# Four attentions in one kernel: another form of nsa's compression, some high halves on ScalarE, and moved steps in swa, diff and fox

## The reference

```
def compress(t, pe, w1, w2):                       # nsa, for keys and for values
    blk = (t[:, :, cidx] + pe).reshape(b, g, n_cmp, CMP_LEN * hd)   # 31 blocks of 32 tokens, step 16
    return jax.nn.gelu(blk @ w1) @ w2              # 2048 -> 256 -> 64
q, k, v, f_logit = jnp.split(x @ w_in, ...)        # fox; log_sigmoid(f_logit + b_f) is summed along the tokens
s = jnp.where(mask, s, -jnp.inf); m = max(s, sink); p = exp(s - m) / (sum + exp(sink - m))   # swa
a = p[:, :, 0] - lam * p[:, :, 1]; o = rms_norm(a @ v)                                       # diff
```

## Time and profile before

| what | value |
|---|---|
| median of three runs | 2526.12 us |
| the profiled execution's own time | 2528.07 us |
| its span | 2526.3 us |
| TensorE busy | 97% |
| GpSimd, VectorE, ScalarE busy | 70%, 54%, 33% |
| mean granted clock of TensorE | 0.993 of full speed |

### The profile page before, as it was taken

The page is one execution under the profiler, slowest core; times in us unless marked ns, Lnnn a source line. Parts: engine busy times, 40 slices in busy tenths (PEclk is TensorE's granted clock), DMA queues, the critical chain, the costliest instruction groups (busy, mean ns, idle before and its releaser), DMA issues. The chain is left out here.

```text
span 2526.3 us, 34447 instructions
## 1 busy us (share of the span) xinstructions
PE 2455.1 (97%) x11904; PEld 2058.3 (81%) x11904; DVE 1354.9 (54%) x2215; ACT 822.2 (33%) x1800; POOL 1774.4 (70%) x1575
## 2 busy tenths in 40 slices
PE   9999999999999999999999999999999999999998
PEld 7888878888887788888888778888877888888886
DVE  7778755666038666663177856444126455633312
ACT  3367742111017731110056643111015554311102
POOL 7866776666667776666689977666666657766664
PEclk9999999999999999999999999999999999999999
DMA  4300012232321132332322212322322221222322
GB/s 145 113 31 26 26 50 95 97 99 92 100 85 58 47 97 93 98 99 96 100 76 67 76 51 84 100 96 95 100 84 68 68 76 59 92 94 97 100 92 83
DMA packets 58695, 208.63 MB, mean 83 GB/s; under 512 B 6560, under 2 KB 7840, under 8 KB 58592
## 3 DMA queue, kind: packets, MB, share of 16 engines
q1 hardware_dynamic: 58320, 206.88, 25.1%
q10 hardware_dynamic: 272, 0.39, 0.0%
HBM read 205.09 MB, written 2.16 MB: 82 GB/s over the span
## 5 line engine op out<-in xcount | busy, mean ns | idle before, releaser
L716 POOL TENSOR_TENSOR WL<-raw,WH 128x1024 fp32r<-128x1024 f32 x380 | 925.8, 2437 | 36.2 <-ACT WH L1989 5.4
L1038 PE MATMUL PS<-HH,WH 128*128 128x512 f32 x2176 | 858.2, 394 | 18.2 <-POOL WL L716 7.0
L1040 PE MATMUL PS<-HH,WL 128*128 128x512 f32 x2176 | 849.8, 391 | 0.0
L1039 PE MATMUL PS<-HL,WH 128*128 128x512 f32 x2176 | 849.7, 390 | 0.0
L1038 PEld LDWEIGHTS PS<-HH,WH 128*128 128x128 f32 x2176 | 409.9, 188 | 110.3 <-issue 9.6
L1040 PEld LDWEIGHTS PS<-HH,WL 128*128 128x128 f32 x2176 | 409.7, 188 | 87.3
L1039 PEld LDWEIGHTS PS<-HL,WH 128*128 128x128 f32 x2176 | 410.2, 189 | 82.3 <-issue 0.5
L704 POOL TENSOR_TENSOR WH<-raw,SC 128x32 fp32r<-128x32 f32 x370 | 107.8, 291 | 473.5 <-DMA raw<-stream 462.3
L705 POOL TENSOR_SCALAR WH<-raw 128x992 fp32r<-128x992 f32 x370 | 394.3, 1066 | 0.0
L1040 PE MATMUL PS<-GH,WL 128*128 (+1 forms) x680 | 264.5, 389 | 0.0
L1038 PE MATMUL PS<-GH,WH 128*128 (+1 forms) x680 | 264.5, 389 | 0.0
(11 more groups left out here) (420 smaller groups left out, 3657.2 us busy)
## 6 DMA issues: line engine op xcount, KB each, us to landing
raw<-stream SPq DMA_DIRECT2D x380, 512.0 KB, 3.6
X<-x SPq DMA_DIRECT2D x4, 512.0 KB, 4.9
out<-X SPq DMA_DIRECT2D x8, 128.0 KB, 1.7
out<-X SPq DMA_DIRECT2D x4, 256.0 KB, 2.0
PR<-params SPq DMA_DIRECT2D x1, 536.0 KB, 8.4
spare_raw_nsa<-stream SPq DMA_DIRECT2D x1, 512.0 KB, 3.6
spare_raw_swa<-stream SPq DMA_DIRECT2D x1, 512.0 KB, 4.4
spare_raw_diff<-stream SPq DMA_DIRECT2D x1, 512.0 KB, 4.4
```

Of the source, the lines that this page charges most:

```text
L716: pool.tensor_tensor(WL[:, w], raw[:, w], WH[:, w].bitcast(F32), ALU.subtract).then_inc(chunk_split, 1)
L1038: pe.matmul(to, h, his[k], start=start and k == 0, stop=False)
L1039: pe.matmul(to, h, los[k], start=False, stop=False)
L1040: last = pe.matmul(to, l, his[k], start=False, stop=stop and k == n_k - 1)
```

## The change

nsa: the compression's operands change sides. `compress(kv, kh)` takes the tokens as the stationary operand and two chunks (both halves of the hidden width) as a moving operand of 2 x 128 columns; it is called four times. The chunk order changes so that these pairs lie side by side. What comes out is tokens x hidden, so ScalarE copies it to `CS`, TensorE turns it (`turn_hidden`, two transposes each time), and GELU reads it from there. The column of the position embedding is one of the 128 tokens' places, filled by `bias_blocks`. ScalarE writes the high halves of chunks 10 to 21. The rotations of nsa's keys and first query read and write PSUM (`rope_in_psum`). Four matmul groups of the second query's projection stand ahead of the first scores. In the loop, `turned_first`, `turned_rest`, `turned_cmp_first`, `turned_cmp_rest` and `total` stand at other places.

swa: ScalarE writes chunk 5's high half, the wait for `q_lo_odd` stands ahead of the second head, the first query's rotation stands ahead of the keys' low half, `evac_q` stands later, two output tiles are one step later.

diff: ScalarE writes the high halves of chunks 3u+7 (u below 6), 24, 25 and 26; the last pair's steps on GpSimd and ScalarE stand in another order. fox: tile 3 goes to PSUM bank 1, its projection doesn't wait for `q_lo`, nor the next for `k_lo`; the forget sums lie in PSUM and are done ahead of q's and k's low halves. Layer norm: `seven_sums` of the right half stands behind that half's products.

```diff
-             ("cmp", 0), ("gate", 0), ("cmp", 1), ("vs", 0), ("cmp", 2), ("vs", 1), ...
+             ("cmp", 1), ("cmp", 3), ("gate", 0), ("vs", 0), ("cmp", 0), ("cmp", 2), ("vs", 1), ("vw", 0), ...
+HIGH_BY_ACT = (10, 22)
 def fox_bank(x):
-    return 0 if x == 2 else proj_bank(x)
+    return {2: 0, 3: 1}.get(x, proj_bank(x))
@@ TensorE, nsa
-                def compress(j):
-                    kv, m, kh = j // 4, j // 2 % 2, j % 2
...
-                    products(c % SLOTS, to, his, los, start=kh == 0, stop=kh == 1
-                             ).then_inc(chunk_used, 1)
+                def compress(kv, kh):
...
+                    pe.wait_ge(chunk_split, c + 2)
+                    to = PS[:, kv, 0:2 * P].rearrange("p (m n) -> p m n", n=P)
+                    for k in range(8):
+                        th, tl = (half[:, kv, k, GROUPS * kh:GROUPS * kh + P] for half in (BLH, BLL))
+                        h, l = WH[:, w:w + 2, k * P:(k + 1) * P], WL[:, w:w + 2, k * P:(k + 1) * P]
+                        pe.matmul(to, th, h, start=kh == 1 and k == 0, stop=False)
+                        pe.matmul(to, th, l, start=False, stop=False)
+                        last = pe.matmul(to, tl, h, start=False, stop=kh == 0 and k == 7)
+                    last.then_inc(chunk_used, 2)
+                def turn_hidden(kv):
+                    pe.wait_ge(cmp_out, kv + 1)
...
+                    for m in range(2):
+                        last = pe.transpose(PS[:, HIDDEN_BANK + kv, m * P:(m + 1) * P], CS[:, m * P:(m + 1) * P], IDF[:])
@@ TensorE, swa's scores
-                        if not nsa and u:
-                            pe.wait_ge(q_lo_odd, u)
+                    if not nsa and h == 1 and u:
+                        pe.wait_ge(q_lo_odd, u)
@@ TensorE, fox
-                    pe.wait_ge(q_lo, before("q_lo", kind) + 1)
                     proj(3)
...
-                            pe.wait_ge(k_lo, before("k_lo", kind) + u + 1)
+                            if u:
+                                pe.wait_ge(k_lo, before("k_lo", kind) + u + 1)
+                            else:
+                                pe.wait_ge(forget_read, 1)
                             proj(3 * u + 4)
@@ TensorE, last_tile
                     if j == 2:
                         seven_sums(k, 0)
                         ln_sums(k, 0)
-                        seven_sums(k, 1)
                     part(1, j)
+                seven_sums(k, 1)
@@ ScalarE
+                def high(x):
...
+                    act.activation(WH[:, w], raw[:, w], ACT.Copy).then_inc(chunk_hi, 1)
@@ GpSimd, diff
                     for u in range(7):
                         cosines_k(u + 1)
-                        split(c, c + 1)
+                        if u == 6:
+                            split_low(c)
+                        else:
+                            split_one(c)
                         cosines_q(u + 1)
...
                             pool.wait_ge(m_mixed, u + 1)
-                            split(c + 1, c + 3)
+                            split_low(c + 1)
+                            split_one(c + 2)
...
                     out_rest(0)
-                    split(last - 2, last - 1)
                     out_rest(1)
                     out_rest(2)
-                    split(last - 1, last)
-                    scale(7, 0)
+                    split_low(last - 2)
                     out_rest(3)
                     out_rest(4)
+                    scale(7, 0)
                     squares_rest(6)
+                    split_low(last - 1)
@@ VectorE, nsa
+                def rope_in_psum(src, scratch, to, out_of, done, k):
...
+                    own.sig(dve.tensor_tensor(WK[:, 3], src, RC[:], ALU.mult))
+                    own.sig(dve.stream_shuffle(scratch, src, swap16))
...
+                    own.link(dve.tensor_tensor(scratch, scratch, RS[:], ALU.mult))
+                    dve.tensor_tensor(to, WK[:, 3], scratch, ALU.add).then_inc(done, 1)
```

More of the change, by code:

```diff
@@ L967, in grouped @@
                 if nsa:
-                    split(q["proj_chunk"] + 3, c)
+                    a, z = (q["proj_chunk"] + x for x in HIGH_BY_ACT)
+                    for x in range(q["proj_chunk"] + 3, c):
+                        if not a <= x < z:
+                            split_high(x)
+                        split_low(x)
                 else:
@@ L979, in grouped @@
                         cosines(u + 1)
+                    if not nsa and m == 0:
+                        split_low(c)
                     if nsa and i == cmp_step(u) + 1:
@@ L1502, in proj @@
                     pe.wait_ge(chunk_split, c0 + x + 1)
[L1503 removed]
+                    bank = fox_bank(x) if fox else proj_bank(x)
+                    products((c0 + x) % SLOTS, PS[:, bank], h_his, h_los).then_inc(chunk_used, 1)
                 def turn_v(u):
@@ L2259, in grouped @@
                     evac_q(1)
+                    high(5)
                 for m in range(8 * per + 2):
                     u, i = divmod(m, per)
+                    early = nsa and 0 < u < 8 and i == cmp_step(u) + 2
+                    late = nsa and i == 3
                     if u < 7 and i == (3 if nsa else 1):
@@ L2284, in grouped @@
                         stack_q(u + 1)
-                    if not nsa and i == 1 and u < 6:
-                        evac_q(u + 2)
+                    if late:
+                        turned_first(m - 1, (0,))
                     if nsa and m >= 3 and m % 2:
@@ L2290, in grouped @@
                         part(m - 2)
-                    if nsa and 0 < u < 8 and i == cmp_step(u) + 2:
-                        turned_first(m - 1, (0,))
-                        turned_cmp_first(u)
+                    if early or late:
                         turned_first(m - 1, (1,))
@@ L2296, in grouped @@
                         turned_first(m - 1, (0, 1))
+                    if not nsa and i == 1 and u < 6:
+                        evac_q(u + 2)
                     if not nsa and m % 2 and m < 8 * per:
@@ L2502, in merged @@
                     v_first(u)
+                    if not more:
+                        normed_first(1)
                     if u:
@@ L3109, in grouped @@
                         cmp_keys_rest()
+                    if nsa and u < 8 and i == cmp_step(u):
+                        masked_cmp(u)
+                    if nsa and m == cmp_step(0) + 2:
+                        turned_cmp_rest(0)
+                    if late:
+                        turned_rest(m - 1, (0,))
+                    if nsa and m >= 3 and m % 2:
+                        total((m - 3) // 2)
+                    if not nsa and m >= 2:
+                        total(m - 2)
+                    if 1 <= m <= 8 * per and not early and not late:
+                        turned_rest(m - 1, (0,))
                     if nsa and 0 < u < 7 and i == 1:
```

223 lines of the change are left out of this document (145 added, 78 removed).

## The result

The changed kernel takes 2507.52 us (median of six runs, 2505.69 to 2512.28), the kernel before 2526.23 us in the same comparison. The ratio is 0.9928, with a 95% interval of 0.9917 to 0.9938: 18.7 us faster, where 44 were forecast and the range ended at 2499 us. The direction was right and the size wrong.

The account below looks back on a forecast made before the run. TensorE, busy 2455.1 of 2526.3 us, was taken as the bound, so only less work or less idle time there could help. The terms summed to -43.95 us, giving 2482 us from 2526.1, range 2470 to 2499 us.

Parts of the forecast that it names:

- compression with the new wait: nsa's compression: 96 matmuls at 0.12 us, -14.3 us; less work covering GELU ahead of its product, +0.8 us.
- nsa's loop: nsa's attention pairs: two of three TensorE waits for low halves go, 1.0 us a pair, six times: -6.0 us.
- swa: Stage swa: shorter waits at the first scores, GpSimd's scaling and the odd head, plus clock: -7.75 us.
- diff's loop: Pairs in diff: a high half leaves the chain that sets the pair's length, six pairs: -3.5 us.
- diff's last pair: End of diff's attention: waits for v's copy, the output's low halves and the mix shrink, clock returns: -6.8 us.
- layer norms: The right half's sums move behind products, into a wait of 0.52 us; 0.5 us, four times: -2.0 us.
- fox: Start of fox: TensorE takes tile 3 earlier, so the first scores come sooner, clock included: -4.4 us.
- the dear compression: Rival in nsa: compression matmuls cost 0.28 us each, 15.4 us more, 2497 us; chance 0.03.
- the late high halves: Rival: ScalarE is late at 22 chunks in nsa, swa and diff, 77 us, giving 2559 us; chance 0.04.
- the ring: diff's loop: GpSimd, VectorE's mix and ScalarE form a cycle of 23.7 us; the change takes a high half out.
- the rival: diff's loop: GpSimd's low half blocks VectorE, 1.3 us a pair, +8 instead of -3.5, 2494 us; chance 0.10.
- The rival of the waits that come back: nsa's loop, swa, diff, layer norm: half of 26 us of waits returns elsewhere, 13 us, 2495 us; chance 0.08.

Follow-up runs that it names:

- n_no_highs: Changed kernel with the high halves of nsa's chunks 10 to 21 on GpSimd again, none on ScalarE there: 2515.46 us, ratio 0.9954.
- n_sines_old: Changed kernel with the next query's shuffle and sines in nsa's loop back at their old place on VectorE: 2502.35 us, ratio 0.9900.
- s_odd_back: Changed kernel with TensorE's wait for the odd head's low half in swa back ahead of the even head's scores: 2509.42 us, ratio 0.9933.
- s_tiles_back: Changed kernel with swa's table of output tiles as in the kernel before: 2506.56 us, ratio 0.9917.
- d_pool_waits: Changed kernel where GpSimd in diff's loop waits for the next pair's q low half before its own low half of chunk 3u+7: 2504.36 us, ratio 0.9909.
- x_four: Changed kernel with nsa's sines back and total between the low halves, swa's old tile table, GpSimd waits for q_lo in diff's loop and last pair: 2493.72 us.
- lf_back: Changed kernel with the layer norms' sums order and fox's VectorE order of q's and k's low halves put back: 2517.32 us, ratio 0.9955.

## Why the prediction was wrong, step by step

Predicted and measured, in us; measured is the step in the table of landmarks, low clock included, and for the layer norms the sum of four steps without the 0.5 us of clock at 1896 us.

| step | predicted | measured |
|---|---|---|
| compression with the new wait | -13.5 | -13.3 |
| nsa's loop | -6.0 | +3.8 |
| swa | -7.75 | -4.0 |
| diff's loop | -3.5 | +1.9 |
| diff's last pair | -6.8 | -3.9 |
| layer norms | -2.0 | -1.1 |
| fox | -4.4 | -4.4 |

- **The compression** was right, in its 0.12 us a matmul and in its size; the dear compression and the late high halves are refuted, and ScalarE's high halves are needed for it (n_no_highs, 8 us).
- **nsa's loop is the step that failed most**: 9.8 us of the 22 missing. The prediction said that the first wait goes "since the low half now stands ahead of the next query's shuffle and sines". That is true of the first low half alone. The second still has shuffle and sines ahead of it, and the values need both. The prediction did not follow it; nor did it see that the sines, moved later, meet GpSimd's cosines (0.5 us), or that `total`, moved ahead of them, waits for ScalarE (0.54 us). Together these put a wait of 1.17 us where one of 0.44 was to go. That cost 5.2 us (n_sines_old), and 1.6 more were low clock at 314 us. The other 3.0 us no run takes apart. Two waits of 0.17 to 0.20 us a pair are new, 0.35 us each with what a wait hides; against them the second wait of the earlier trace rows, which the prediction left, went too.
- **swa**: the first scores gave 1.3 us as predicted, the scaling 0.6 of 1.5, and the clock 1.5 at 779 to 783 us (taken 1.7; the mean granted clock over 117 us is 0.99 now and was 0.97). The wait for the odd head's half was to give 3.25 us and gave 0.8 until 822 us and next to nothing at 825.57 (s_odd_back), since VectorE's low halves of the turned block are late there. Another 1.5 us came ahead of 822 us without a cause that a run shows. And a part of the diff was not priced at all: the tiles that stand one step later bring a wait of 2.44 us, 1.1 us net (s_tiles_back).
- **diff's loop**: the ring did get shorter, and the rival happened too. Without the collision a pair is 0.7 us shorter than before (23.0 against 23.7), so the -3.5 us stood on a right mechanism; the blocked VectorE takes 1.05 us of it a pair. The rival's own sum, 1.3 us a pair on top of the old length, counted the collision as if the ring stayed: the truth has both, +0.3 us. It had been given a chance of 0.10. The Trainium skill, "SBUF — State Buffer", section "Who interferes with whom", has the rule for it (two SBUF inputs on VectorE against a reading GpSimd instruction, exclusive for the whole instruction); the trace agrees, with 2.77 us for 0.69, and with d_pool_waits. The row that spoke for it lay in the prediction's own rows. Diff's loop in the kernel before had such a meeting too, once a pair, at the sines L3184, which take 0.69 us at 1319.20 us. Timelines of GpSimd and VectorE in the kernel before:

```profile
1346.18 2.40 POOL L716 TENSOR_TENSOR WL<-raw,WH 128x1024 fp32r<-128x1024 f32 x1
...
1346.32 2.80 DVE L3184 TENSOR_TENSOR WK<-WK,RS 128x512 f32<-128x512 f32 x1
```

- **diff's last pair**: of the waits of the earlier trace rows the first fell from 2.92 to 0.89 us and the others went, but three came, read from a timeline of TensorE in the changed kernel:

```profile
1437.42 0.66 PE L1543 MATMUL PS<-IDF,WK 128*128 128x128 f32 x4 [0.89 <-ACT WK L2456]
1439.15 1.09 PE L1588 MATMUL PS<-IDF,PC 128*128 128x128 f32 x8 [1.07 <-DVE PC L3370]
...
1442.05 0.39 PE L1567 MATMUL PS<-MKH,MQ 128*128 128x256 f32 x1 [1.81 <-DVE MQ L3328]
...
1456.06 1.09 PE L1588 MATMUL PS<-IDF,PC 128*128 128x128 f32 x8 [1.26 <-DVE PC L3370]
```

  The mixes are late next, as was said, but by 2.3 us and not 0.5; and q's low half, 1.81 us where 0.49 was, meets GpSimd's low halves of the output, which the change put there. What the collision alone costs there was only tried together with other edits: in x_four this wait is 0.85 us, and the last pair ends 0.8 us earlier against its start.
- **Layer norms**: a term of the right kind, mis-sized by about half: of 0.5 us each 0.2 to 0.4 came, since behind the sums ScalarE's L2007 is late (1.06 us where 0.66 was).
- **fox** was right in its size, with 1.6 us of the 4.4 being low clock that the trace before had at 1913 us and that the sum had counted in. It was not for TensorE's order alone: with the forget sums behind the low halves it would have lost more than it won (lf_back).
- **The rival of the waits that come back** had 0.08 and 2495 us. It was nearest to the truth in kind: swa's and the last pair's waits had others behind them. That half of 26 us comes back was too little: by the table 3.3 us of the 26 were won. But not all of the rest is a wait that was there already and came to light. In nsa 5.2 us are the new order, and in diff's loop the collision of VectorE and GpSimd is new.
- The median lies 1.8 us above the profiled execution, and 1.0 us of its gain came ahead of the compression. Both were outside the prediction's sum.

## What to carry to other kernels

When one instruction is moved ahead of another, write down the new place of everything on that engine between the two places, and price the ones that moved back. A wait on TensorE that hangs on VectorE goes for good only if VectorE's own sequence up to the last product that is waited for gets shorter; in nsa it got 1.05 us longer. And when GpSimd gets a long instruction next to a short VectorE one with both inputs in SBUF, order them by a wait: starting GpSimd's 1.5 us later gave 1 us a pair here.

## What the runs showed of the hardware

- Several VectorE instructions with all inputs in SBUF were held while a GpSimd instruction that reads SBUF ran, and ended 0.3 to 1.1 us behind it: L3328 (2.77 us for 0.69), L3184 (2.80), nsa's sines (1.28 for 0.76), the scan of the earlier trace rows, L3327 in the last pair (1.20 us), and in the kernel before in the cast of the forget sums, beside L716 from 1918.47 us:

```profile
1918.82 2.33 DVE L2591 CAST FRH<-WK 16x512 fp32r<-16x512 f32 x1
```

- With an input in PSUM these two were not held. VectorE in the changed kernel, while GpSimd's L725 runs from 1895.67 to 1898.07 us:

```profile
1895.97 1.22 DVE L3293 TENSOR_TENSOR_SCAN PS<-WK,PS 16x512 f32<-16x512 f32 x1
1897.22 0.68 DVE L2694 CAST FRH<-PS 16x512 fp32r<-16x512 f32 x1
```

  The scan took 3.28 us in the earlier trace rows and the cast 2.33 us; here they take 1.22 and 0.68.
- Some waits are followed by some us at the low clock and some are not, and the length of the wait does not tell them apart here. In the changed kernel the low clock came behind waits of 1.00 us (at 313.99 us) and 2.19 us (825.57), and not behind those of 2.26 us (138.23) and 2.44 us (844.18). In n_sines_old, in the place of the one of 2.26 us, the windows show:

```profile
138.00:143.00 5.00, 4.46 (x15) 3.49 (x16) 0.49 (x1) 1.03 (x2) 4.82 (x8) 0.66 0.00 0
```

  The mean of 0.66 says that part of the stretch ran at the low level (1.2 GHz), where matmuls of 512 columns stand 0.43 us apart instead of 0.23. What decides between them was not tried. It costs 1.6 us there. At 19 to 25 us, where nothing of this change is near, it cost the kernel before 2.8 us, most of which a wait of 1.97 us in the changed kernel evened out.
